# Gate and up projections of the feed-forward layers: 18 of 22 pairs in a seven-product block form

## The reference

```python
def rmsnorm(x, g):
    xf = x.astype(jnp.float32)
    y = xf * lax.rsqrt(jnp.mean(xf * xf, axis=-1, keepdims=True) + EPS)
    return (y * g.astype(jnp.float32)).astype(x.dtype)

def ffn_half(h, g_pre, g_post, w_in, w_out):
    a = rmsnorm(h, g_pre) @ w_in
    gate, up = jnp.split(a, 2, axis=-1)
    return h + FFN_RESID * rmsnorm((jax.nn.silu(gate) * up) @ w_out, g_post)
```

## Time and profile before

| | |
|---|---|
| timed runs | 2434.26, 2437.1, 2438.48 us; median 2437.1 |
| span of the profiled execution | 2438.0 us |
| its own time | none is given apart from the span |
| TensorE busy | 2378.5 us (98%) |
| VectorE, ScalarE, GpSimd busy | 828.6, 784.9, 834.6 us (34%, 32%, 34%) |
| granted TensorE clock, mean | 0.994 of full |
| moved from and to HBM | 220.29 MB, 90 GB/s |

### The profile page before, as it was taken

One profiled execution on the slowest core, in us unless ns is written; L12 is line 12 of the kernel. 1 busy time (PEld: TensorE's weight loads), 2 busy tenths in 40 slices (PEclk: granted clock), 3 DMA queues, 4 the chain that ended last, 5 costly groups with the idle time before them and its releaser, 6 DMA issues.

```text
span 2438.0 us, 39450 instructions
## 1 busy us (share of the span) xinstructions
PE 2378.5 (98%) x15328; PEld 2158.4 (89%) x15328; DVE 828.6 (34%) x1877; ACT 784.9 (32%) x1586; POOL 834.6 (34%) x441
## 2 busy tenths in 40 slices
PE   8999999999889999999999999999999999999998
PEld 8999988986556899998889999888999789999987
DVE  4223300586421533330053232004565644232101
ACT  5223212614322632322252322224422444222222
POOL 3333333240312333333324333331344223333332
PEclk9999999999998999999999999999999999999999
DMA  3222222232671222222222222222211432222222
GB/s 122 83 83 81 94 78 87 69 108 79 195 237 52 73 84 82 82 94 79 87 70 87 78 86 86 87 79 79 77 57 53 148 95 79 79 86 80 93 82 86
DMA packets 74906, 220.29 MB, mean 90 GB/s; under 512 B 9405, under 2 KB 26302, under 8 KB 74527
## 3 DMA queue, kind: packets, MB, share of 16 engines
q1 hardware_dynamic: 71710, 208.09, 26.8%
q0 software_dynamic: 3072, 10.49, 1.3%
HBM read 210.73 MB, written 7.82 MB: 90 GB/s over the span
## 4 chain that ended last, share of the span: by engine, by line
PE 86%; DVE 4%; SPq 3%; ACT 3%; issue 2%; DMA 2%; POOL 1%; DVEq 0%; ACTq 0%; POOLq 0%
PE psum L1758 18%; PE psum L1760 18%; PE psum L1759 18%; PE psum L1890 7%; PE psum L1892 7%; PE psum L1891 7%; PE psum L1883 2%; PE psum L1884 2%; SPq L442 1%; PE psum L2244 1%; ACT y L665 1%; SPq L493 1%; DVE y L1190 1%; SPq L458 1%; PE psum L2162 1%
## 5 line engine op out<-in xcount | busy, mean ns | idle before, releaser
L1047 POOL TENSOR_TENSOR w_lo<-raw,w_hi 128x1024 fp32r<-128x1024 f32 (+1 forms) x317 | 759.0, 2397 | 1378.4 <-ACT w_hi L651 1378.3
L1758 PE MATMUL psum<-x_hi,w_hi 128*128 128x320 f32 (+1 forms) x3312 | 986.2, 298 | 0.7 <-POOL w_lo L1047 0.5
L1760 PE MATMUL psum<-x_hi,w_lo 128*128 128x320 f32 (+1 forms) x3312 | 981.2, 296 | 0.0
L1759 PE MATMUL psum<-x_lo,w_hi 128*128 128x320 f32 (+1 forms) x3312 | 981.2, 296 | 0.0
L1758 PEld LDWEIGHTS psum<-x_hi,w_hi 128*128 128x128 f32 x3312 | 629.9, 190 | 4.0 <-POOL w_lo L1047 1.9
L1759 PEld LDWEIGHTS psum<-x_lo,w_hi 128*128 128x128 f32 x3312 | 629.9, 190 | 0.2
L1760 PEld LDWEIGHTS psum<-x_hi,w_lo 128*128 128x128 f32 x3312 | 629.7, 190 | 0.0
L651 ACT ACTIVATE w_hi<-raw 128x1024 fp32r<-128x1024 f32 (+1 forms) x323 | 339.9, 1054 | 828.5 <-DMA raw<-ffn_out 375.9
L1268 DVE TENSOR_TENSOR work<-psum,r_pre 128x256 f32<-128x256 f32 (+1 forms) x352 | 160.3, 457 | 660.4 <-PE psum L1760 658.2
L1890 PE MATMUL psum<-w_hi,gu_hi 128*128 128x512 f32 x704 | 275.0, 391 | 0.6
L1891 PE MATMUL psum<-w_hi,gu_lo 128*128 128x512 f32 x704 | 274.0, 389 | 0.0
(11 more groups left out here) (274 smaller groups left out, 2077.7 us busy)
## 6 DMA issues: line engine op xcount, KB each, us to landing
raw<-ffn_in SPq DMA_DIRECT2D x176, 512.0 KB, 3.6
raw<-ffn_out SPq DMA_DIRECT2D x88, 512.0 KB, 3.5
raw<-gla_in SPq DMA_DIRECT2D x25, 512.0 KB, 3.6
cache<-cache POOLq DMA_DIRECT2D x64, 160.0 KB, 5.2
cache<-cache SPq DMA_DIRECT2D x64, 160.0 KB, 5.4
c_k<-cache_kt SPq DMA_DIRECT2D x64, 128.0 KB, 3.4
raw<-mla_wo SPq DMA_DIRECT2D x8, 512.0 KB, 3.6
raw<-gla_wo SPq DMA_DIRECT2D x8, 512.0 KB, 3.6
```

What stands on the lines that cost most here:

```text
L1047: pool.tensor_tensor(w_lo[slot][:, 0:w], raw[slot][:, 0:w], w_hi[slot][:, 0:w].bitcast(F32), ALU.subtract).then_inc(s_lo, 1)
L1758: pe.matmul(out, wh, xh, start=start, stop=False)
L1759: pe.matmul(out, wh, xl, start=False, stop=False)
L1760: return pe.matmul(out, wl, xh, start=False, stop=stop)
```

## The change

Pairs 0 to 3 stay as they were (`CLASSIC = 4`). The other 18 become groups. A pair's weights are a matrix of 2 x 2 quarters of 128 columns by 512 features: a11 and a12 are the gate's, a21 and a22 the up's. The tokens are 2 x 2 blocks of 512 features by 288 tokens. Seven products instead of eight make the four results of 128 x 288. Four use sums of weight quarters (s1 = a21 + a22, s2 = s1 + a11, s4 = s2 + a12, s3 = a11 + a21; signs are kept in the token forms and at the evictions), three use token forms made once a stage (`t_f`, in the place of `h`).

- TensorE (`group`, `product`): products 1 to 6, in the order a11, s1, s2, s4, s3, a12, are 4 k tiles x 3 matmuls of 288 columns; the seventh, a22, is 4 plain float32 matmuls. Banks `b_a` and `b_c` hold sums of several products. Before a further product is added, ScalarE copies out what is there (`copy_out`).
- ScalarE makes the high parts of a11, a12 and the four sums, three copies out of PSUM, two silus and two high parts of the result.
- VectorE makes the sums and their low parts for the next group, adds the copies to the banks, and applies `r_pre` to the gate only (`scaled`). The up half keeps its tokens' factor out; the post-norm of the stage takes the factor away again, and its epsilon is scaled by `h_q`, made from the tokens' sums of squares. The classic pairs do likewise: `gate_up` multiplies straight from the bank.
- GpSimd makes only the low parts of a11 and a12 (128 x 512).
- SP loads four quarters of 256 KB a group (`four`), a12 and then a21 and a11 of the next group once the one before is used up.
- `h` goes to a buffer `keep` in DRAM at a stage's start, and comes back (from the input in the first stage) behind the first four loads of output weights. `y_biases`, `update` and `pre_factors` wait for it or use `h_q`.
- Loops (`Fori`) are written out, several semaphores are merged, also in the mixers, and `gu` holds high and low parts in one tile.

```diff
+CLASSIC = 4
+GRP = FT - CLASSIC
...
+                    if st > 0 and j == SLOTS - 1:
+                        for t in ORDER:
+                            sp.wait_ge(s_hnew, updated(st, t))
+                            sp.dma_start(keep[t, 0:rows_in(t), :], row(t)).then_inc(f_keep, 16)
...
+                def four(g, i):
+
+                    a = g0 + g
+                    if g >= 2:
+                        sp.wait_ge(f_p, 7 * (a - 1) + 14 * i)
+                    part(w[f"a22_{g % 2}"], 1, 1, f_a2[g % 2], g, i)
+                    sp.wait_ge(f_sum, 4 * (a - 1) + 3 + 8 * i)
+                    sp.wait_ge(f_alo, 2 * a + 4 * i)
+                    part(w["a12"], 0, 1, f_a12, g, i)
+                    sp.wait_ge(f_sum, 4 * a + 8 * i)
+                    part(w["a21"], 1, 0, f_a2[g % 2], g, i)
+                    part(w["a11"], 0, 0, f_a11, g, i)
...
+
+                n = 7 * (g0 + GRP - 1)
...
+                for t in ORDER:
+                    src = io["x_t"] if st == 0 else keep
+                    sp.dma_start(row(t), src[t, 0:rows_in(t), :]).then_inc(f_back, 16)
...
+                def copy_out(dst, src, a, order, i):
+                    act.wait_ge(f_p, 7 * a + order + 14 * i)
+                    act.activation(dst[:, :], src[:, 0:HALF], ACT.Copy).then_inc(f_e, 1)
...
+                    if g > 0:
+                        last_half(g - 1, i)
+                    hi_sum("s3", a, 4, 5, i)
+                    if g > 0:
+                        high_part(g - 1, c_1[(g - 1) % 2], 2 * a, 0, i)
+                    if a >= 2:
...
+                        act.wait_ge(s_gulo, c0 + 2 * a)
...
+                        act.wait_ge(f_gu, 2 * a - 1 + 4 * i)
+                    copy_out(c_3, ring(st, g, 1), a, 2, i)
+                    if a >= 1:
+                        act.wait_ge(s_gulo, c0 + 2 * a - 1 + 4 * i)
+                    copy_out(c_2, ring(st, g, 0), a, 3, i)
...
+                def part_low(name, a, order, used, i):
+                    pool.wait_ge(f_hi, 6 * a + order + 12 * i)
+                    if a > 0:
+                        pool.wait_ge(f_p, 7 * (a - 1) + used + 14 * i)
+                    pool.tensor_tensor(w[f"{name}_lo"][:, :], w[name][:, :], w[f"{name}_hi"][:, :].bitcast(F32),
+                                       ALU.subtract).then_inc(f_alo, 1)
...
+                    if stages[b - 1] == "ffn":
+                        last = dve.scalar_tensor_tensor(out=y_bias[0:r, c], in0=y_ss[0:r, 0, c], scalar=resid_scale(b),
+                                                        in1=h_q[0:r, c], op0=ALU.mult, op1=ALU.add)
...
+
...
+                    dve.tensor_tensor(c[:, :], ps[:, 0:HALF], c[:, :], ALU.add).then_inc(f_c, 1)
+
...
+                    a = g0 + g
+                    dve.wait_ge(s_silu, c0 + 2 * a + 2 + 4 * i)
+                    dve.wait_ge(f_p, 7 * a + 7 + 14 * i)
+                    c = c_1[g % 2]
+                    dve.scalar_tensor_tensor(out=c[:, :], in0=ring(st, g, 0)[:, 0:HALF], scalar=-1.0, in1=c[:, :], op0=ALU.mult,
...
+                def group(g, i, more):
+                    a = g0 + g
+                    if g > 0:
+                        last_half(g - 1, i)
+                    low_form("s4", g, 4, 3, i)
+                    if g > 0:
+                        low_part(g - 1, c_1[(g - 1) % 2], 2 * a, 0, i)
+                    low_form("s3", g, 6, 4, i)
+                    if g == 0:
+                        x_low_form(1, 3)
+                    if more:
+                        sum_1(g + 1, i)
+                    plus(c_2, ring(st, g, 1), a, 3, 4, i)
+                    scaled(c_2, 1, 5 * a + 1, i)
+                    if more:
+                        sum_2(g + 1, i)
+                    dve.wait_ge(f_e, 3 * a + 2 + 6 * i)
+                    dve.wait_ge(f_p, 7 * a + 5 + 14 * i)
+                    dve.scalar_tensor_tensor(out=c_3[:, :], in0=ring(st, g, 0)[:, 0:HALF], scalar=-1.0, in1=c_3[:, :], op0=ALU.mult,
+                                             op1=ALU.subtract).then_inc(f_c, 1)
+                    dve.wait_ge(s_silu, c0 + 2 * a + 1 + 4 * i)
+                    dve.wait_ge(f_c, 5 * a + 3 + 10 * i)
+                    dve.tensor_tensor(c_2[:, :], c_2[:, :], c_3[:, :], ALU.mult).then_inc(f_gu, 1)
+                    if more:
+                        low_form("s1", g + 1, 2, 2, i)
+                        sum_4(g + 1, i)
+                    plus(c_1[g % 2], ring(st, g, 2), a, 1, 6, i)
+                    scaled(c_1[g % 2], 0, 5 * a + 4, i)
+                    if more:
+                        sum_3(g + 1, i)
+                    low_part(g, c_2, 2 * a + 1, 1, i)
+                    if more:
+                        low_form("s2", g + 1, 3, 3, i)
+
...
+                def product(out, name, x, fresh):
+
+                    for k in range(HK):
+                        c = slice(k * P, (k + 1) * P)
+                        hi, lo = w[f"{name}_hi"][:, c], w[f"{name}_lo"][:, c]
+                        for y, m, first, end in ((hi, x[0], k == 0, False), (hi, x[1], False, False), (lo, x[0], False, k == HK - 1)):
+                            last = pe.matmul(out[:, 0:HALF], y, m[:, k, :], start=fresh and first, stop=end, skip_group_check=not fresh)
...
+                    b_a, b_c, b_b = (ring(st, g, j) for j in range(3))
+                    if g < 2:
+                        pe.wait_ge(s_evicted, u0 + 4 * CLASSIC - RING + 3 * g + 3)
+                    pe.wait_ge(f_alo, 2 * a + 1 + 4 * i)
+                    if g >= 2:
+                        pe.wait_ge(f_gu, 2 * (a - 1) + 4 * i)
+                    product(b_a, "a11", b_11, True)
+                    pe.wait_ge(f_lo, 4 * a + 1 + 8 * i)
+                    if g >= 2:
+                        pe.wait_ge(f_c, 5 * (a - 2) + 1 + 10 * i)
+                    if g == 0:
+                        pe.wait_ge(f_tlo, 3 * f + 1)
+                    product(b_c, "s1", t_1, True)
+                    pe.wait_ge(f_lo, 4 * a + 2 + 8 * i)
+                    pe.wait_ge(f_e, 3 * a + 1 + 6 * i)
+                    if g == 0:
+                        pe.wait_ge(f_tlo, 3 * f + 2)
+                    product(b_a, "s2", t_2, False)
+                    pe.wait_ge(f_lo, 4 * a + 3 + 8 * i)
+                    pe.wait_ge(f_e, 3 * a + 2 + 6 * i)
+                    product(b_c, "s4", b_22, False)
+                    pe.wait_ge(f_lo, 4 * a + 4 + 8 * i)
+                    pe.wait_ge(f_e, 3 * a + 3 + 6 * i)
+                    if g == 0:
+                        pe.wait_ge(f_tlo, 3 * f + 3)
+                    product(b_a, "s3", t_3, False)
+                    pe.wait_ge(f_alo, 2 * a + 2 + 4 * i)
+                    if g >= 2:
+                        pe.wait_ge(f_c, 5 * (a - 2) + 4 + 10 * i)
+                    product(b_b, "a12", b_21, True)
+                    pe.wait_ge(f_c, 5 * a + 3 + 10 * i)
+                    pe.wait_ge(f_a2[g % 2], 32 * (GRP // 2 * f + g // 2 + 1) + 32 * i)
+                    if g == 0:
+                        pe.wait_ge(f_x, 8 * f + 8)
+                    for k in range(HK):
```

More of the change, by code:

```diff
@@ L48 @@
 GROUPS = PAGES // 4
-SP_PAGES = 2
 CACHES = 4
@@ new lines, in ffn @@
+                classic_out(sp, st, 0)
+                wait_keep(sp, st)
+                part(w["a21"], 1, 0, f_a2[0], 0, 0)
+                part(w["a22_0"], 1, 1, f_a2[0], 0, 0)
+                part(w["a11"], 0, 0, f_a11, 0, 0)
+                classic_out(sp, st, 2)
+                part(w["a12"], 0, 1, f_a12, 0, 0)
+                classic_out(sp, st, 3)
+                four(1, 0)
+                for i in range((GRP - 2) // 2):
+                    four(2, i)
+                    four(3, i)
@@ L567, in mla @@
+                sp.dma_start(g_post[:, :], io["post_g"][st]).then_inc(s_g, 16)
+                for i in range(SLOTS, FO):
+                    load(b0 + FB + i, w_out[f, i // (FT // 2), i % (FT // 2)])
             def mla(st):
@@ L780, in ffn @@
+                group(0, 0, True)
+                for i in range((GRP - 2) // 2):
+                    group(1, i, True)
+                    group(2, i, True)
+                group(GRP - 1, 0, False)
+                last_half(GRP - 1, 0)
+                split(b0 + FB + 1)
+                high_part(GRP - 1, c_1[(GRP - 1) % 2], 2 * (g0 + GRP), 0, 0)
+                split(b0 + FB + 2)
                 out_phase(st)
@@ new lines, in sum_4, with sum_3, low_form @@
+                def sum_4(g, i):
+                    a = g0 + g
+                    dve.wait_ge(f_sum, 4 * a + 2 + 8 * i)
+                    dve.wait_ge(f_a12, 16 * (a + 1) + 32 * i)
+                    add("s4", "s2", "a12", a, 4, i)
+                def sum_3(g, i):
+                    add("s3", "a11", "a21", g0 + g, 5, i)
+                def low_form(name, g, hi, summed, i):
+                    a = g0 + g
+                    dve.wait_ge(f_hi, 6 * a + hi + 12 * i)
+                    dve.wait_ge(f_sum, 4 * a + summed + 8 * i)
```

(23 more changed lines are left out.)

502 lines of the change are left out of this document (340 added, 162 removed).

## The result

| | before | with the change |
|---|---|---|
| median of 4 runs | 2437.79 us (2434.26 to 2443.21) | 2425.19 us (2419.83 to 2426.68) |
| ratio | | 0.9936, 95% interval 0.9916 to 0.9956 |
| span of the profiled execution | 2438.0 | 2424.8 |
| mean granted clock | 0.994 | 0.991 |
| TensorE, VectorE, GpSimd busy | 98, 34, 34% | 95, 55, 28% |

The change saves 12.6 us of 2438 by the medians. (The quotient of the medians is 0.9948, the ratio in the table 0.9936; the interval holds both.) The groups stand 12.25 us apart, where 12.35 was forecast; 51 of the 68 distances within a stage lie between 12.24 and 12.26.

The account below looks back on a forecast made before the run. Before the change only matmul time counts; after it, a loop through VectorE, ScalarE and TensorE at 12.35 us a group. Saving 32 us, less 20 for the entries, gives 12 off the 2438.0 span: 2425 us, range 2400 to 2462.

Parts of the forecast that it names:

- The loop: Product 3 waits for ScalarE's copy, queued behind VectorE's last product of the group before: 12.35 us a group; 57%.
- the sign of being right: What would confirm the forecast in the trace: among others, groups 12.3 to 12.4 us apart.
- VectorE's run: VectorE's 14 instructions from plus_2 to last_half: 6.87 us, 8.0 with the delays by GpSimd's subtractions.
- Products 3 and 4: TensorE's piece of the cycle: 24 matmuls of 288 columns and the handoff to VectorE, 3.4 us.
- The port: VectorE instructions on SBUF are held up by a running GpSimd subtraction: 1.08 us by a12's low part, 0.05 by a11's.
- TensorE's part: TensorE alone needs 11.54 us a group instead of 12.8: 91 us over 72 groups, the most to win.
- The entry: VectorE makes the tokens' block forms between pair 1 and the first group: 5 us lost a stage, 20 in all.
- until the cycle is in step: A piece of the loss at each stage's start, after product 3 of the first group: another 1.3 us.
- Late weights: Rival, 20%: quarter loads past 4.2 us delay a11's subtraction onto VectorE's sums, each 0.1 us costing 7 over 72 groups.
- GpSimd did not wait for the port: Rival, 15%, said it waits: a12's low part starts at last_half, a PSUM instruction; cycle about 12.2, time 2414.
- Costed at nothing: Storing and reading back the residual, leaving the norm factor off the up half, and merged mixer semaphores add no time.
- The norm factor on the up half: Leaving it off takes no instruction off the path, since it was VectorE's, which idled: nothing gained.

Follow-up runs that it names:

- e2: Changed kernel with two of the seventh product's four float32 matmuls left out: 2421.11 us, groups still 12.25 us apart.
- e1: Changed kernel with VectorE's last product of a group (last_half) moved ahead, right behind sum_3: 2397.05 us, groups 12.02 us apart.
- e7: Changed kernel with ScalarE's copy of product 1's bank moved ahead of the previous group's last high part: 2403.18 us, groups 12.02 us apart.
- e10: Changed kernel with one more VectorE instruction a group, multiplying the up half's last result by r_pre too: 2457.02 us, groups 12.75 us apart.
- e3: Changed kernel with GpSimd writing zeros into a12's low part in place of the subtraction: 2377.58 us, groups usually 11.65 us apart, uneven.
- e5: Changed kernel with last_half moved right behind sum_3 and a21, then a11, loaded ahead of a12: 2360.35 us, groups 11.49 us apart.
- e9: Changed kernel with ScalarE's copy ahead of the high part and a21 loaded first, VectorE's order kept: 2359.79 us, groups 11.49 us apart.
- e4: Changed kernel with SyncE loading a21, then a11, ahead of a12: 2412.56 us, usual distance of groups 12.25 us.
- e8: Changed kernel with the residual not stored, each stage reading back x_t instead: 2426.91 us, ratio 0.9932 to the kernel before.

## Why the prediction was right

Forecast 2425, measured 2425.19, and not by luck of two errors, at least in the large terms:

- **The loop.** Forecast 12.35, measured 12.25. The usual distance lies just under the 12.3 to 12.4 given as the sign of being right, the mean (12.32) within. TensorE loses 0.70 ahead of product 3, by the starts, where about 0.8 was said. VectorE's run 8.0, measured 7.79: two of the pairs of dependent instructions were dearer in the sum than in the trace (plus_2 to scaled is 0.49, and the other one 0.48, where end plus 0.11 was counted). ScalarE 0.95, measured 0.93. Products 3 and 4 3.4, measured 3.53: the first matmul after the stall takes 0.21 to the next instead of 0.13, and the handoff 0.11 instead of 0.03. e2 shows that it is a loop beside TensorE, e1 and e7 show its two queues, e10 that an instruction put on it counts in full.
- **The port.** 1.08 a group forecast, 1.04 shown by e3, which took 2377.58.
- **TensorE's part.** 11.54 forecast; 11.49 in e5 and e9. The seventh product takes 1.72 (186.44 to 188.16), and the first matmul behind it 0.2 more than usual, together the 1.93 forecast. (The row gives 2.91 us for 1728 columns, 1.68 ns a column where 1.67 was written; that moves the sum by 0.02.)
- **The entry.** 5 us a stage forecast; 4.9, 4.0, 3.7 and 7.0 measured up to the first seventh product (against the classic pairs' pace and six products), 19.6 in all for 20. The parts were less well seen. Product 1 comes 1.0 us late for 1.7; product 3 at 32.0 after pair 2's start for 32.5. What was not in the sum is the wait for a21 of the second group: VectorE waited 1.7 to 3.9 us for it, and the seventh product of the first group for VectorE, 3.60 us in stage 4 (rows below). That and its echo are part of what I had called "until the cycle is in step".

TensorE and VectorE of the change, stage 4:

```profile
2065.93 4.21 PE L2353 MATMUL psum<-t_f,a_r 128*128 128x288 f32 x8 [3.60 <-DVE c L1636]
```

```profile
2062.28 0.69 DVE L1563 TENSOR_TENSOR s_r<-a_r,a_r 128x512 f32<-128x512 f32 x1 [3.94 <-DMA a_r<-ffn_in]
```

- **The account.** 72 x 0.55 = 39.6, less 19.6 for the entries, less 4.8 for groups longer than 12.25, makes 15.2. The four stages, from first unit to first output matmul, give 3.2, 5.2, 5.1 and 1.6: 15.1. Another 2 us are lost between the stages, 1.1 of them around the gated linear attention. That stretch varies by as much from kernel to kernel (468.1 to 472.2 us, 471.1 before), and I don't lay it to the change. So a gain some 7 us larger than forecast (39.6 for 32) met losses of about the same size that were not in the sum: 4.8 and 2. To that extent the 0.2 us between forecast and result is chance.
- **The rivals.** Late weights were given 20% and a slope of 7 us for each 0.1. That rival did not come as told, but its mechanism did in small: 17 of 68 distances are longer than 12.27. Three of these (12.76, 12.77, 13.51) are the first of a stage, behind the entry; in the one shown a quarter's lateness reaches VectorE through GpSimd and the port; the others weren't traced to a cause. In e4, with a21 and a11 loaded earlier, 5 are left. GpSimd did not wait for the port until a PSUM instruction: in all but six cases it takes 1.28 to 1.36 us and VectorE gives way. The six are at the entries, 1.63 to 1.74 us, and the one looked at waited for a single VectorE instruction (the last section). No row of any run has GpSimd reading or writing PSUM.
- **Costed at nothing.** The residual: storing it shown by e8, reading it back by the output matmuls' time. The norm factor on the up half: wrong in kind. Leaving it off was called free because VectorE had idled before; in the new loop it is worth 0.49 us a group (e10), 32 us by the medians. The forecast doesn't suffer by this, since its loop was summed without that instruction.
